# Triangular inverses on four 64x64 tiles of TensorE instead of two

## The reference, cut to what matters

```
X  = (A T) masked to the blocks below the diagonal, of this level
T  = T - T X          (the inverse for blocks of twice the size)
```

## Time and profile before

| | |
|---|---|
| median of 3 runs | 4079.07 us (4078.73 to 4081.39) |
| the profiled execution: span of the core | 4078.9 us |
| TensorE busy | 3830.4 us, 94% of the span |
| VectorE busy | 2658.7 us, 65% |
| ScalarE, GpSimd busy | 1344.8 us and 1193.2 us |
| mean granted clock of TensorE | 0.960 |
| the eight inverses lie between | 2860 and 3605 us of the span |

### The profile page before, as it was taken

How to read it: one execution, slowest core, us unless ns; L and a number is a source line. 1 busy time by engine, 2 the same in 40 slices (tenths; PEclk the granted TensorE clock), 3 DMA queues, 4 the chain that set the end, 5 groups by cost and what they waited for, 6 DMA issues and landing times.

```text
span 4078.9 us, 51857 instructions
## 1 busy us (share of the span) xinstructions
PE 3830.4 (94%) x20718; PEld 3011.2 (74%) x20718; DVE 2658.7 (65%) x3054; ACT 1344.8 (33%) x1764; POOL 1193.2 (29%) x578
## 2 busy tenths in 40 slices
PE   8999999999889998999999989999999989999998
PEld 7567788877666766778887767887677767776777
DVE  7964878789865553487878888533545554546783
ACT  5242432244433333242324343212222131324512
POOL 2012044445213332114444422223122221212064
PEclk9999999999889999999999989999989989899999
DMA  3002232354311010223326332223211221323053
GB/s 112 21 26 84 106 108 93 110 181 149 121 68 37 32 37 26 93 98 116 101 92 209 129 133 101 94 104 117 83 56 54 74 78 63 116 75 106 28 205 145
DMA packets 131770, 385.58 MB, mean 95 GB/s; under 512 B 13565, under 2 KB 14209, under 8 KB 126281
## 3 DMA queue, kind: packets, MB, share of 16 engines
q1 hardware_dynamic: 131528, 382.27, 26.8%
HBM read 281.00 MB, written 101.22 MB: 94 GB/s over the span
## 4 chain that ended last, share of the span: by engine, by line
PE 71%; DVE 22%; ACT 3%; issue 2%; POOL 1%; DMA 1%; DVEq 0%; SPq 0%; ACTq 0%; POOLq 0%
PE ps L380 22%; PE ps L1453 21%; PE ps L476 8%; PE ps L2976 3%; PE ps L4489 2%; PE ps L907 2%; PE ps L2250 1%; DVE acc L1722 1%; PE ps L2242 1%; DVE top L1626 1%; DVE xop L1626 1%; PE ps L3077 1%; DVE x L661 1%; PE ps L4153 1%; DVE t L641 1%
## 5 line engine op out<-in xcount | busy, mean ns | idle before, releaser
L333 POOL TENSOR_TENSOR wlo<-wraw,whi 128x1024 fp32r<-128x1024 f32 x181 | 446.9, 2469 | 1772.4 <-ACT whi L325 1763.8
L1453 PE MATMUL ps<-xop,whi 128*128 128x512 f32 x1984 | 618.1, 393 | 14.3 <-DVE acc L1747 9.6
L325 ACT ACTIVATE whi<-wraw 128x1024 fp32r<-128x1024 f32 x185 | 196.1, 1060 | 921.3 <-PE ps L380 610.9
L1453 PE MATMUL ps<-top,whi 128*128 128x512 f32 x1488 | 468.3, 396 | 19.7 <-DVE acc L1716 15.9
L1453 PEld LDWEIGHTS ps<-xop,whi 128*128 128x128 f32 x1984 | 373.0, 188 | 99.3 <-DVE acc L1747 12.1
L1453 PE MATMUL ps<-xop,wlo 128*128 128x512 f32 x992 | 388.1, 391 | 0.0
L476 PE MATMUL ps<-xhalf,whi 128*128 128x512 f32 x1024 | 374.0, 448 | 0.3 <-POOL wlo L333 0.3
L1453 PEld LDWEIGHTS ps<-top,whi 128*128 128x128 f32 x1488 | 280.6, 189 | 87.6 <-DVE acc L1716 19.0
L1851 POOL TENSOR_TENSOR wlo<-wsum,whi 128x1024 fp32r<-128x1024 f32 (+2 forms) x102 | 229.1, 2246 | 362.7 <-ACT whi L1478 362.4
L380 PE MATMUL ps<-xhi,whi 128*128 128x512 f32 x868 | 307.0, 435 | 20.7 <-DVE xlo L681 9.1
L1453 PE MATMUL ps<-top,wlo 128*128 128x512 f32 x744 | 293.5, 394 | 0.0
(11 more groups left out here) (637 smaller groups left out, 7132.8 us busy)
## 6 DMA issues: line engine op xcount, KB each, us to landing
wraw<-in_w_dram SPq DMA_DIRECT2D x185, 512.0 KB, 3.5
h_keep<-h SPq DMA_DIRECT2D x154, 256.0 KB, 4.5
wraw<-in_s_dram SPq DMA_DIRECT2D x48, 512.0 KB, 4.1
f<-h_keep SPq DMA_DIRECT2D x24, 768.0 KB, 5.5
wmore<-in_s_dram SPq DMA_DIRECT2D x32, 512.0 KB, 4.0
x_keep<-x SPq DMA_DIRECT2D x16, 1024.0 KB, 3.8
g_keep<-gates SPq DMA_DIRECT2D x64, 256.0 KB, 2.4
gb<-g_keep SPq DMA_DIRECT2D x32, 512.0 KB, 3.7
```

Of the source, the lines that this page charges most:

```text
L325: se.own().activation(K.hi(c), K.raw[:, c % NRAW, :], ACT.Copy).then_inc(*K.S(("hi", c)))
L333: ge.own().tensor_tensor(K.lo(c), K.raw[:, c % NRAW, :], K.hi(c).bitcast(F32), SUB).then_inc(*K.G(("lo", c)))
L1453: d = pe.e.matmul(out[:, s, :], w[:, o], x[:, i, :], start=(j < 3 and i == 0 and t == 0), stop=(i == k - 1 and t == 2), skip_group_check=True)
```

## The change

The running transpose `I.TC` now lies in the other 64 partitions: the transpose of the upper block of each matrix in BOTTOM, that of the lower block in TOP. So A and T are read from one half of the partitions, while the product that needs them is written to the other half (`ACROSS`), and the masked `I.X` lies there too, next to the `I.TC` that it is multiplied with. In the tt group each half p then issues two products on the same operands: T X goes to the other half o, and the transposed product to the half p. The tt group's order is, for every e: TOP to BOTTOM, TOP to TOP, BOTTOM to TOP, BOTTOM to BOTTOM. These are all four combinations of a half of the rows and a half of the columns of the array, where the order before used two of them. The two results T X and its transpose have a bank each; the x group has one bank, written by both halves. At level 6 the eight matrices are split into two times four: four go TOP to BOTTOM, and four TOP to TOP, then BOTTOM to TOP and TOP to TOP. The number of products is the same everywhere. VectorE's halves become whole 128x512 operations, with one more subtraction at level 5.

```diff
-        for i in range(4):
-            two = ((TOP, 4 * h + i), (BOTTOM, 4 * (1 - h) + i))
-            yield from two if h == 0 else two[::-1]
+ACROSS = ((TOP, BOTTOM), (BOTTOM, TOP))
...
+    def across(b, lhs, rhs):
+        for e in range(8):
+            for p, o in ACROSS:
+                d = mm(K.ps[o, b, part(e, 64)], lhs(p, e), rhs(p, e), start=True, stop=True, skip_group_check=True)
         return d
...
     for k in range(1, 6):
-        bs = [take(pe, K, Q, n, "x", k, s) for s in range(2)]
+        b = take(pe, K, Q, n, "x", k)
         pe.wait_ge(*K.at(n, "t", k - 1))
-        product(I.A, I.T, 0, bs).then_inc(*K.T((n, "x mm", k)))
-        yield
-        bs = [take(pe, K, Q, n, "t", k, s) for s in range(2)]
+        across(b, lambda p, e: I.A[p, e, p], lambda p, e: I.T[p, e, :]).then_inc(*K.T((n, "x mm", k)))
+        yield
+        bt, bc = (take(pe, K, Q, n, name, k) for name in ("t", "tt"))
         pe.wait_ge(*K.at(n, "tt", k - 1))
         pe.wait_ge(*K.at(n, "x", k))
-        product(I.TC, I.X, 0, bs)
-        product(I.X, I.TC, 1, bs).then_inc(*K.T((n, "tt mm", k)))
+        for e in range(8):
+            for p, o in ACROSS:
+                mm(K.ps[o, bt, part(e, 64)], I.TC[p, e, :], I.X[p, e, :], start=True, stop=True, skip_group_check=True)
+                d = mm(K.ps[p, bc, part(e, 64)], I.X[p, e, :], I.TC[p, e, :], start=True, stop=True, skip_group_check=True)
+        d.then_inc(*K.T((n, "tt mm", k)))
...
-    for e in range(8):
-        d = mm(K.ps[BOTTOM, b, part(e, 64)], I.A[TOP, e, BOTTOM], I.T[TOP, e, :], start=True, stop=True, skip_group_check=True)
+    for e in range(4):
+        for o, f in ((BOTTOM, e), (TOP, e + 4)):
+            d = mm(K.ps[o, b, part(e, 64)], I.A[TOP, f, BOTTOM], I.T[TOP, f, :], start=True, stop=True, skip_group_check=True)
...
-    for e in range(8):
-        d = mm(K.ps[TOP, b, part(e, 64)], I.X[BOTTOM, e, :], I.TT[BOTTOM, e, BOTTOM], start=True, stop=True, skip_group_check=True)
+    for e in range(4):
+        mm(K.ps[TOP, bs[0], part(e, 64)], I.X[BOTTOM, e, :], I.TT[BOTTOM, e, BOTTOM], start=True, stop=True, skip_group_check=True)
+        d = mm(K.ps[TOP, bs[1], part(e, 64)], I.X[TOP, e, :], I.TC[TOP, e + 4, :], start=True, stop=True, skip_group_check=True)
...
-        for s in range(2):
-            ve.own().tensor_tensor(I.X[:, part(s, 4), :], inverse_half(K, n, "x", k, s, 0), mask, MUL).then_inc(*V((n, "x", k), ("free", (n, "x", k, s))))
+        mask = H.level[k].unsqueeze(1).to_broadcast([128, 8, 64])
+        ve.own().tensor_tensor(I.X, e8(K.bank(n, "x", k)), mask, MUL).then_inc(*V((n, "x", k), ("free", (n, "x", k))))
...
+        ve.own().tensor_tensor(I.T[rows], I.T[rows], e8(K.bank(n, "t", k))[rows], SUB).then_inc(*V((n, "t", k), ("free", (n, "t", k))))
+        tt = e8(K.bank(n, "tt", k))
+        if k < 5:
+            ve.own().tensor_tensor(I.TC, I.TC, tt, SUB).then_inc(*V((n, "tt", k), ("free", (n, "tt", k))))
+        else:
+            for p, o in ACROSS:
+                ve.own().tensor_tensor(I.TT[p, :, p], I.TC[o], tt[o], SUB).then_inc(*V())
+            ve.own().tensor_tensor(I.TC[TOP, 4:8, :], I.TC[TOP, 4:8, :], tt[TOP, 4:8, :], SUB).then_inc(*V((n, "tt", k), ("free", (n, "tt", k))))
```

More of the change, by code:

```diff
@@ L2958, in e8 @@
     return x.rearrange("p (a b) -> p a b", a=8)
[L2961 to L2966 removed]
+ACROSS = ((TOP, BOTTOM), (BOTTOM, TOP))
 def inverse_tensor(pe, K, Q, n, I):
     mm = pe.e.matmul
[L2973 to L2976 removed]
+    def across(b, lhs, rhs):
+        for e in range(8):
+            for p, o in ACROSS:
+                d = mm(K.ps[o, b, part(e, 64)], lhs(p, e), rhs(p, e), start=True, stop=True, skip_group_check=True)
         return d
[L2979 removed]
+    b = take(pe, K, Q, n, "turn")
     pe.wait_ge(*K.at(n, "tt", 0))
[L2981 to L2983 removed]
+    across(b, lambda p, e: I.TC[p, e, :], lambda p, e: K.ident[p, p]).then_inc(*K.T((n, "turned")))
     yield
     for k in range(1, 6):
[L2986 removed]
+        b = take(pe, K, Q, n, "x", k)
         pe.wait_ge(*K.at(n, "t", k - 1))
[L2988 removed]
+        across(b, lambda p, e: I.A[p, e, p], lambda p, e: I.T[p, e, :]).then_inc(*K.T((n, "x mm", k)))
         yield
[L2990 removed]
+        bt, bc = (take(pe, K, Q, n, name, k) for name in ("t", "tt"))
         pe.wait_ge(*K.at(n, "tt", k - 1))
         pe.wait_ge(*K.at(n, "x", k))
[L2993 to L2994 removed]
+        for e in range(8):
[3 more added lines that the diff above has]
+        d.then_inc(*K.T((n, "tt mm", k)))
         yield
@@ L3016, in inverse_first @@
 def inverse_first(ve, K, H, n, I):
-    for p in (TOP, BOTTOM):
+    for p, o in ACROSS:
         mask = H.level[0][p].unsqueeze(1).to_broadcast([64, 8, 64])
-        ve.own().tensor_tensor(I.TC[p, :, :], I.A[p, :, p], mask, MUL).then_inc(*K.V())
+        ve.own().tensor_tensor(I.TC[o, :, :], I.A[p, :, p], mask, MUL).then_inc(*K.V())
     ve.own().tensor_tensor(I.TC, H.ident64.unsqueeze(1).to_broadcast([128, 8, 64]), I.TC, SUB).then_inc(*K.V((n, "tt", 0)))
-def inverse_half(K, n, name, k, s, at):
-    return K.bank(n, name, k, s)[:, part(at, 256)].rearrange("p (a b) -> p a b", a=4)
 def inverse_vector(ve, K, H, n, I):
@@ L3038, in inverse_vector @@
         ve.wait_ge(*K.at(n, "tt mm", k))
-        for s in range(2):
-            T = I.T[rows, part(s, 4), :]
-            ve.own().tensor_tensor(T, T, inverse_half(K, n, "t", k, s, 0)[rows], SUB).then_inc(*V((n, "t", k)))
-        for s in range(2):
-            tt, TC = inverse_half(K, n, "t", k, s, 1), I.TC[:, part(s, 4), :]
-            if k < 5:
-                ve.own().tensor_tensor(TC, TC, tt, SUB).then_inc(*V((n, "tt", k), ("free", (n, "t", k, s))))
-            else:
-                for p in (TOP, BOTTOM):
-                    ve.own().tensor_tensor(I.TT[p, part(s, 4), p], TC[p], tt[p], SUB).then_inc(*V((n, "tt", k), ("free", (n, "t", k, s))))
+        ve.own().tensor_tensor(I.T[rows], I.T[rows], e8(K.bank(n, "t", k))[rows], SUB).then_inc(*V((n, "t", k), ("free", (n, "t", k))))
[3 more added lines that the diff above has]
+        else:
+            for p, o in ACROSS:
+                ve.own().tensor_tensor(I.TT[p, :, p], I.TC[o], tt[o], SUB).then_inc(*V())
+            ve.own().tensor_tensor(I.TC[TOP, 4:8, :], I.TC[TOP, 4:8, :], tt[TOP, 4:8, :], SUB).then_inc(*V((n, "tt", k), ("free", (n, "tt", k))))
         yield
@@ L3055, in inverse_scalar @@
     se.wait_ge(*K.at(n, "turned"))
-    for s in range(2):
-        se.own().activation(I.T[:, part(s, 4), :], K.bank(n, "turn", s)[:, 0:256].rearrange("p (a b) -> p a b", a=4), ACT.Copy).then_inc(*K.S((n, "t", 0), ("free", (n, "turn", s))))
+    se.own().activation(I.T, e8(K.bank(n, "turn")), ACT.Copy).then_inc(*K.S((n, "t", 0), ("free", (n, "turn"))))
     yield
@@ L3060, in inverse_scalar @@
     se.wait_ge(*K.at(n, "x mm", 6))
-    se.own().activation(I.X[BOTTOM, :, :], e8(K.bank(n, "x", 6))[BOTTOM], ACT.Copy).then_inc(*K.S((n, "x", 6), ("free", (n, "x", 6))))
+    se.own().activation(I.X[:, 0:4, :], e8(K.bank(n, "x", 6))[:, 0:4, :], ACT.Copy).then_inc(*K.S((n, "x", 6), ("free", (n, "x", 6))))
     yield
     se.wait_ge(*K.at(n, "tt mm", 6))
-    se.own().activation(I.TT[TOP, :, BOTTOM], e8(K.bank(n, "tt", 6))[TOP], ACT.Copy, scale=-1.0).then_inc(*K.S((n, "inverse"), ("free", (n, "tt", 6))))
+    for s in range(2):
+        se.own().activation(I.TT[TOP, part(s, 4), BOTTOM], e8(K.bank(n, "tt", 6, s))[TOP, 0:4, :], ACT.Copy, scale=-1.0).then_inc(*K.S((n, "inverse"), ("free", (n, "tt", 6, s))))
     yield
```

13 lines of the change are left out of this document (1 added, 12 removed).

## The result

The changed kernel takes 4032.65 us (median of 4 runs, 4021.20 to 4040.97). The kernel before took 4055.54 to 4081.39 beside it; the ratio is 0.9887 with a 95% interval of 0.9863 to 0.9912, 46 us less (36 to 56). The forecast was 4038, "faster", with a range from 4024 to 4066. The same kernel timed again on another occasion gave 4027.5 (4005.39 to 4037.76, 6 runs), ratio 0.988 (0.9848 to 0.9912).

What follows compares the result with a forecast made beforehand. TensorE, through the inverse's products on its own chain, was taken as the bound. 41 + 8 = 49 us, times 0.91 is 45, plus 2 VectorE, minus 1 issue, minus 5 swallowed: 41 us, so 4038 from 4078.9; range 4024 to 4066.

Steps and rivals of the forecast that it cites:

- The factor of two in the tt groups: Inverse's levels 1 to 5: four tiles side by side take 1.15 us per group instead of 2.08, 37 us at full clock.
- The rival of a shared path for the weights: Column tiles share the weights' path, so tt groups save nothing: 4075, no change that can be told; chance 0.08.
- Issue: TensorE's tt groups: a product takes some 0.036 us to issue, so groups starting with an empty queue lose 1 us in all.
- The bound of 0.05 us per product: Rival: issue at the windows' upper edge limits tt groups to 1.6 us, saving only 11 us there: 4062; chance 0.10.
- The bank shared by both halves of the rows: x groups and turn: both row halves write one PSUM bank; priced at nothing, x groups staying at 1.15 us.
- The slower rival, 4114: Row halves cannot write one bank together, so x groups and turns take 2.08 us instead of 1.15: +35 us; chance 0.05.
- Half clock: tt groups running at half clock: half of their extra 8 us is saved too, 4 us.
- Level 6: Both product groups of the inverse's last level use two tiles instead of one: 8 us of TensorE saved.
- the swallowed part: Savings lost to the other stream's parallel VectorE chain: minus 5 us; as a rival, half of 49 lost, 4055, chance 0.12.
- the share on the chain: Part of the inverse products' TensorE time on the path that sets the end: 0.91, turning 49 us into 45.
- VectorE's whole operations: Inverse's half operations become whole ones, 0.69 us instead of 0.85 per pair, shortening TensorE's waits: 2 us, bounds 0 and 5.
- the wait for L3045: TensorE waited nine times, 3.3 us in all, because this VectorE operation freed the x group's second bank; one bank removes it.

Runs made afterwards that it cites:

- e1: Changed kernel with the last products of a level ordered as before, all 16 for T, then 16 for its transpose: 4052.85 us, ratio 0.9941 to before.
- e5: Changed kernel plus seven probe blocks of products on one, two and four tiles ahead of each inverse batch's turn: 4203.04 us in one run.
- e3: Changed kernel with VectorE's whole 128x512 operations of the inverse split into halves of 128x256 again: 4020.85 us, ratio 0.9868 to before.
- e9: Changed kernel with the last products of levels 1 to 5 issued four times, in bursts of 256 records: 4193.51 us in one run.
- e2: Changed kernel with level 6 on one tile as before, including its ScalarE copies and VectorE's last level 5 operations: 4021.95 us, ratio 0.987 to before.
- e8: The changed kernel itself, unedited, timed and profiled again on another occasion: 4027.5 us, ratio 0.988 to before.
- e4: Changed kernel with the last products of levels 1 to 5 issued twice, same order and places: 4062.52 us, ratio 0.9970 to before.

## Why the prediction was right, point by point

**The factor of two in the tt groups** held: 1.864 to 0.943 us first to last, 40 x 0.92 = 37 us at full clock, the predicted figure. e1 shows that the interleaved order does it, and e5 that tiles of the same rows load and multiply beside each other as L3986 in the earlier trace rows had it. The rival of a shared path for the weights falls. A rule of the Trainium skill speaks against it, too: "TensorE: Matmul & The Clock Gate" (section "The mechanism") says that weight loads overlap matmuls in flight only where the row group differs. Taken so, the same-row block of e5 would have stood near the 3.7 us of one tile (an estimate from that rule and the first block), and it took 1.8.

**Issue.** One microsecond was set aside for slow starts on an empty queue, 9 in the range. The two tt groups of e3 that began so took 0.943 us like the others, so the term is nothing. The 0.036 us between the first two loads in the earlier trace rows was misread as the time that each product takes to issue: it stands once, at the start (e3), and the group that it was read from took 1.863 us first to last like all the others of before. The bound of 0.05 us per product was not the right shape either: a burst of 64 or 128 records runs at 0.015 us a record, and the limit shows only further on (e5, e9). The floor of 25 ns between starts that the Trainium skill gives ("TensorE: Matmul & The Clock Gate", section "Wait — 56ns, not 53.3ns?") does not hold across tiles: in the first 0.02 us of a group four records start, and over it one starts every 0.015 us on average.

**The bank shared by both halves of the rows** costs nothing where they write different partitions: x groups 0.930 us in both kernels, the crossed block of e5 1.70. The slower rival, 4114, would have needed 2 us there. "TensorEngine Tiling (Array Packing)" of the Trainium skill (section "Gotcha 1: PSUM Pressure") forbids such a pair the same bank at one time; these rows show no sign of it. No run had both halves write the same partitions of one bank at once.

**Half clock.** 4 us more were expected for groups at half clock; the trace of the changed kernel has 42.5 us for all tt groups where before had 82.8, 40.3 saved against 41. But the prediction did not say that the end moves by 10 to 20 us from run to run with the clock, more than any term but the first.

**Level 6.** The mechanism was right on TensorE, 0.92 to 0.46 us and 7.4 us in all. At the end 8 x 0.91 = 7 was put; e2 gives the edit back and loses 4 to 5.5 us over its runs, with a standard error of up to 2. The term was a little large, if anything.

**VectorE, the swallowed part and the share on the chain.** For VectorE's whole operations 2 us were put, with bounds 0 and 5, and e3 has 3 to 5 (standard error 2). Their length was right. The reason given for a part of it was not: the wait for L3045 of the earlier trace rows was put down to the x group's second bank, and it comes back in e3, where the x group has one bank and VectorE's operations are halves. The 5 us to be swallowed were not: TensorE's idle time between the first turn and the last level 6 went from 43.6 to 38.9 us, 44.0 in e8. And 0.91 understates the path a little: e1 and e4 have 31 for 30 and 40 for 37 us of work, the whole of it within the error. These terms, each a few us too low, make the difference: 37 + 7.4 = 44 of TensorE, 49 by the reckoned span over all runs, 46 by the timed ones, 41 predicted.

**What stays open**: the split of the 5 us between TensorE's 44 and the 49. VectorE's part by e3 would fill most of it, but its error is nearly half as large. How much of level 6's 7.4 us reaches the end. And why TensorE's stream of records is late at the second border of 256, which no run varied.

## What to carry to other kernels

Where small products of one kind can go to another half of rows or columns, put the operands so that all four 64x64 tiles have work and issue them in turn, one per tile: order alone was worth 30 us of TensorE here, and all of it reached the end because the products lay on TensorE's own chain. Read beforehand what else waits there: the pair products, woven in the same way, took less TensorE time and mostly turned into a wait for VectorE. Keep such a burst short: 64 and 128 records ran through, 256 did not. And compare kernels of this size by span times granted clock before a cause is sought for 20 us, over several runs each: by one profile each e2 and e3 looked free, and the mean of their runs says otherwise.

## What the runs showed of the hardware that was not expected

- A float32 64x64 tile takes a record every 0.058 us whether 64, 32 or 16 columns are moved, and whichever other tiles work (e5).
- Four tiles at 0.015 us a record outrun what feeds TensorE: bursts of 64 and 128 records between slower work show no stall, of 40 bursts of 256 records 36 do, 1.5 us each on average (55.6 / 36). The stalls lie whole multiples of 256 records of matmuls and loads apart, through all that stands between (e5, e9).
- Products move across the change from one pair of tiles to another: 32 records on one pair and then 32 on the other take 1.69 us first to last, not 1.87 (e1).
- On an empty queue only the first weight load of a group stands alone, 0.036 us ahead of the next; after it they follow as with a full queue (e3).
- Two profiles of the same program differed by 23 us of span, 4039.2 and 4016.1, and by 2 us of span times clock; over 35 runs of the kernel before the product still spreads by 16 us, 3906 to 3922.
